# Hybrid decoder block on 8 cores: which pass over a weight tile leaves its bf16 copy behind

## The chip, the cores and the metric

One Trainium2 chip, all 8 of its cores. Each core works on 2 of the 16 sequences and no core waits for another, but they share the chip's memory. The time is device microseconds of the slowest core; a kernel's time is the median of its runs. Cores 0 to 3 are one die, 4 to 7 the other.

## The reference, cut to what matters

```python
def reference(x, meta_tokens, ...):          # x (16, 2048, 1024) float32
    h = concatenate([meta, x], axis=1)
    u = rms_norm(h, norm_mix_g) @ w_in       # (1024, 2576)
    c_val, c_gate, q, k, v, g, gate_lr = split(u)   # 512 512 256 256 512 512 16
    y_conv = silu(layer_norm(causal_conv31(c_val * sigmoid(c_gate))))
    y_gla = gated_linear_attention(q, k, v, decay(gate_lr))   # 4 heads, chunks of 64
    y_gla = head_norm(y_gla) * silu(g)
    h = h + concatenate([y_conv, y_gla], -1) @ w_out          # (1024, 1024)
    h = h + (silu(r @ w_gate) * (r @ w_up)) @ w_down, r = rms_norm(h, norm_ffn_g)   # 1024 -> 2816 -> 1024
    return rms_norm(h, norm_final_g)[:, 16:]
```

## The kernel before

A core's 4096 tokens are cut into 8 **blocks** of 512. A block goes through a mixer (`mixer`: convolution group, attention group, output projection) and a feed-forward part (`ffn`: 22 column groups j of gate and up, then the down projection). The feed-forward of a block is interleaved with the second part of the next block's mixer and the first part of the mixer after that. `plan` orders these pieces (`side` spreads them over a block by shares), each piece adds its instructions to `Prog`, and `Prog.schedule`, a list scheduler with estimated costs, sets the order on each engine by rank and readiness. After that each engine runs its list strictly in order. The queues of SyncE (SP) and GpSimd (POOL) also issue the DMAs: an instruction there that waits for a semaphore holds up all behind it.

**Weights.** All of them, 48 tiles of 128 x 2048, lie in memory as f32 (`wpack`, 1 MB a tile) and don't fit on chip, so each block loads every tile again, in a bf16 form of 512 KB in a slot of `wring`. Ring 0 (slots 0 to 3) serves the mixer (v, k, q, output gate, output projection; later the conv tiles too), ring 1 (slots 4 to 7) the feed-forward, and in block 0 the two first tensors of `h[2]` hold k and q (ring 2: wring8 and 9, printed as h_0 and h_1 or h2_0 and h2_1). `wget` hands out a slot, `wdone` frees it, and the freed slot is at once reloaded with the next tile of that ring's sequence (`wissue`). A reload waits for the last reader of the slot, be it TensorE or a store.

**Three kinds of load.** (a) A *cast*: GpSimd's queue reads the f32 tile and writes bf16 into the slot. (b) A cast followed by a *store*: SP's queue writes the slot to the bf16 copy `wsc` in memory. (c) A *read*: SP's queue reads `wsc`, once there is a copy. Tiles of `LATE_STORE` are cast twice and stored after the second cast; the others are cast once and stored at once. Tile numbers: 0 to 3 conv, 4 q, 5 k, 6 and 7 v, 8 and 9 output gate, 10 to 13 output projection, 14 to 24 gate (FG0 to FG10), 25 to 35 up (FU0 to FU10), 36 to 47 down (FD0 to FD11). Groups j = 2i and 2i+1 use FGi and FUi.

**Block 0.** The conv tiles' stores are put aside in `held_in` and written in the unit `ln`, after the convolution (`Bycv`). The tiles of rings 0 and 2 have a list `hold` of their own.

Lines that the rows name: L677 all products of eight steps (`mm8`: projections and gate/up; in the rows `ps<-x2T,wring` is gate/up, `ps<-wring,xT` v or output gate, `ps<-wring,yT` the output projection, `ps<-xT,wring` k, q or conv), L1297 the down projection, L449 a cast, L446 a read, L456 a store, L1249 the load of a block's tokens into `h`, L1333 the store of a finished block, L813 and L818 the way of the convolution's input through `vsc` into `rep`, L925 to L929 and L1024 GpSimd's part of the layer norm, L1122 its part of the attention state.

Of the kernel before, what the change touches and what calls it, by code (L numbers as in the profile page):

```python
# [28 lines left out]
NW = NWM + NWF  # L29
# [4 lines left out]

W_GATE, W_VAL, W_Q, W_K, W_V, W_G, W_O, W_FG, W_FU, W_FD = 0, 2, 4, 5, 6, 8, 10, 14, 25, 36
N_WT = 48
LATE_STORE = frozenset(t for t in range(N_WT) if W_Q <= t < W_O or (t >= W_FG and t % 3))

ORDER = (("start xt0 xt1 xt2 xt3 mt c0 c1 rep0 c2 c3 rep1 wcv z decay v0 v1 v2 v3 vm km conv0 k conv1 q ln g0 g1 g2 g3",
# [237 lines left out]
def build_program(nseq, seqlen):  # L277
# [25 lines left out]
    with es:  # L303
# [68 lines left out]
        def build(wseq):  # L372

            P = Prog()
            Bh = [[Buf(f"h{s_}_{t}") for t in range(NT)] for s_ in range(NH)]
# [32 lines left out]
            Bw = [Buf(f"w{i}") for i in range(NW)] + Bh[2][0:NWX]  # L408
# [26 lines left out]
                return ftmp[i], Bft[i]  # L435


            order, stored, loaded, freed, once = ([], [], []), set(), [0, 0, 0], (set(), set(), set()), set()
            RING = ((0, NWM), (NWM, NWF), (NW, NWX))

            def wissue(r, n, after=(), hold=None):
                tile, sl = wseq[r][n], RING[r][0] + n % RING[r][1]
                B_ = Bw[sl]
                dst = wring[sl][:]
                if tile in stored:
                    op = P.add("sp", lambda e: e.dma_start(out=dst, in_=wsc[tile]), R=[Bwsc[tile]], W=[B_], dkey=f"wh{sl}")  # L446
                    op.rank = (P.rank - 30.0, op.rank[1])
                else:
                    P.add("pool", lambda e: e.dma_start(out=dst, in_=wpack[tile]), R=after, W=[B_], dkey=f"wp{sl}")  # L449
                    if tile in LATE_STORE and tile not in once:  # L450
                        once.add(tile)
                        return
                    stored.add(tile)

                    def write(after=()):
                        P.add("sp", lambda e: e.dma_start(out=wsc[tile], in_=dst), R=[B_], A=after, W=[Bwsc[tile]], dkey=f"ws{sl}")  # L456
                    if hold is None:
                        write()
                    else:
                        hold.append(write)  # L460
# [13 lines left out]
            def wdone(o):  # L474

                if wseq is None:
                    return
                r = o.ring
                freed[r].update(range(o.first, o.first + len(o)))
                while loaded[r] in freed[r]:  # L480
                    n = loaded[r]
                    loaded[r] += 1
                    if n + RING[r][1] < len(wseq[r]):
                        wissue(r, n + RING[r][1])
# [3 lines left out]
            held_in, conv_w = [], {}  # L488

            def cload(dst, src, eng="sp", key=None):  # L490
                ncst[0] += 1
                P.add(eng, lambda e: e.dma_start(out=dst, in_=src), W=[Bc2(dst)], dkey=key or ("const" + eng))
# [19 lines left out]
                      W=[Bh[0][t]], dkey=f"h0_{t}")  # L512
            gain(gmix, g_mix_d, "gm")
            if wseq is not None:
                hold = []
                for r, n in [(1, 0), (1, 1), (1, 2), (1, 3)]:
                    wissue(r, n, after=[Bh[0][1]], hold=held_in)
            cload(wgl[:], wglp_d, eng="pool")
            if wseq is not None:
                for r, n in [(0, 0), (0, 1), (0, 2), (0, 3), (2, 0), (2, 1)]:  # L520
                    wissue(r, n, after=[Bh[0][1]], hold=hold)
                for write in hold:
                    write([Bw[NW + 1]])
            cload(wg2[:], wg2_d)
            cload(gb[:], gb_d)
            cload(convw4[:], convw4_d)
# [872 lines left out]
            n = sum(c for c, _ in pre)  # L1399
# [3 lines left out]
            n = sum(c for c, _ in post + late)  # L1403
# [5 lines left out]
            for b in range(nb):  # L1409
                units, fin = ffn(b % NH, blocks[b][0], b == 0, b == nb - 1)  # L1410
                n = sum(c for c, _ in units)
# [17 lines left out]
            return P, order  # L1429

        _, wseq = build(None)
        P, _ = build(wseq)
        nc.model_us = P.schedule()
        P.finalize()
# [95 lines left out]
```

How the kernel before makes its waits and increments, by code:

```python
    def emit(self, eng_name, eng, esem, dsem):  # L241
        seen = {}
        for b in self.ops[eng_name]:
            waits = {}
            for a in b.deps:
                if not self._needs_wait(a, b):
                    continue
                if a.dma:
                    s, v = dsem[a.dkey], (self.dcount[a.dkey] if a.dkey.startswith("const") else a.dval)
                else:
                    s, v = esem[a.eng], a.ticket
                k = id(s)
                if k not in waits or waits[k][1] < v:
                    waits[k] = (s, v)
            for k, (s, v) in waits.items():
                if seen.get(k, 0) >= v:
                    continue
                seen[k] = v
                eng.wait_ge(s, v)
            if b.fn is None:
                continue
            ins = b.fn(eng)
            if b.dma:
                ins.then_inc(dsem[b.dkey], 16)
            elif b.sig:
                ins.then_inc(esem[eng_name], 1)
```

## Time and profile before

| what | value |
|---|---|
| time, median of 3 runs (lowest, highest) | 1532.19 us (1531.98, 1574.51) |
| the profiled execution's own time, and its span | 1533.17 us, 1531.6 us |
| spans of the 8 cores | 1511.4 to 1531.6 us |
| TensorE busy; idle under L677 for casts, for reads (core 4) | 1433.6 us; 12.0 us, 8.6 us |
| DMA issues: casts, reads, stores of weight tiles | 77 (75 + 2 into `h[2]`), 303, 48 |
| to landing, median: cast, read, store | 9.5, 5.0, 6.1 us |
| memory read, written by one core | 276.22 MB, 46.40 MB |

The profile is of one execution and, without a core named, of core 4, whose span is the longest. The own time is 1.6 us over the span. "x31" is a count of instructions, a number in brackets the idle time before, with what ended it.

### The profile page before, as it was taken

How to read it: one execution, taken by the hardware profiler on the slowest of the kernel's cores; microseconds unless marked ns; L12 is line 12 of the kernel's file. 1: busy time of each engine (PE TensorE's matmuls, PEld its weight loads, DVE VectorE, ACT ScalarE, POOL GpSimd, SP SyncE). 2: the span in 40 equal slices, each digit the busy share in tenths (PEclk: the TensorE clock that was granted, in tenths of full speed). 3: DMA queues.
4: the chain of work that ended last, by engine and by line, in shares of the span. 5: the costliest groups of instructions: out<-in, count | busy, mean ns of one | idle time of the engine just before them, and what ended most of it. 6: DMA issues, size and time to landing. Idle time of an engine off the chain costs nothing.

```text
span 1531.6 us, 26341 instructions; the slowest of 8 cores (1511.4 to 1531.6 us)
## 1 busy us (share of the span) xinstructions
PE 1433.6 (94%) x8203; PEld 688.0 (45%) x8290; DVE 792.0 (52%) x1751; ACT 549.6 (36%) x976; POOL 266.5 (17%) x359
## 2 busy tenths in 40 slices
PE   4977899988999999999999999999999999999995
PEld 2444444434444444444444444444444444444442
DVE  3586275434654347545384356643484455744424
ACT  3654352434324344214523154223442145211102
POOL 2241240114201141002400133001410014000000
PEclk9989999999999999999999999999999999999998
DMA  9868997999878974497745985489744985375541
GB/s 193 215 169 197 184 212 172 203 236 258 215 208 236 247 227 150 146 219 241 213 145 173 210 273 166 147 200 232 244 154 143 219 239 174 114 211 178 187 163 55
DMA packets 128568, 297.55 MB, mean 194 GB/s; under 512 B 49056, under 2 KB 59680, under 8 KB 128432
## 3 DMA queue, kind: packets, MB, share of 16 engines
q1 hardware_dynamic: 66000, 199.92, 41.5%
q0 software_dynamic: 23904, 86.49, 25.8%
q10 hardware_dynamic: 38528, 9.44, 4.9%
q8 instruction: 70, 1.15, 0.3%
q14 instruction: 66, 0.54, 0.1%
HBM read 276.22 MB, written 46.40 MB: 211 GB/s over the span
## 4 chain that ended last, share of the span: by engine, by line
PE 79%; DMA 10%; issue 4%; ACT 4%; DVE 2%; POOL 0%; SPq 0%; DVEq 0%; ACTq 0%; POOLq 0%
PE ps L677 57%; PE ps L1297 17%; DMA wring<-wsc 4%; DMA wring<-wpack 4%; ACT yT L635 1%; PE ps L656 1%; PE ps L764 1%; PE ps L875 1%; DMA h<-xin 1%; DMA out<-h 1%; ACT rep L1030 0%; PE ps L1171 0%; PE ps L1198 0%; PE ps L1166 0%; PE ps L1069 0%
## 5 line engine op out<-in xcount | busy, mean ns | idle before, releaser
L677 PE MATMUL ps<-x2T,wring 128*128 128x512 bf16 (+1 forms) x2912 | 640.8, 374 | 21.7 <-DMA wring<-wsc 8.6
L677 PEld LDWEIGHTS ps<-x2T,wring 128*128 128x128 bf16 x2912 | 277.9, 98 | 345.7 <-issue 34.1
L1297 PE MATMUL ps<-wring,actT 128*128 128x512 bf16 x1368 | 305.6, 379 | 3.2 <-DMA wring<-wpack 1.0
L1281 DVE SCALAR_TENSOR_TENSOR ftmp<-ftmp,ps 128x512 f32<-128x512 f32 x176 | 120.7, 686 | 253.6 <-ACT ftmp L1280 253.3
L1280 ACT ACTIVATE ftmp<-ps 128x512 f32<-128x512 f32 x176 | 105.3, 599 | 353.4 <-PE ps L677 337.3
L1297 PEld LDWEIGHTS ps<-wring,actT 128*128 128x128 bf16 x1408 | 136.7, 98 | 168.7 <-issue 8.8
L677 PE MATMUL ps<-xT,wring 128*128 128x512 bf16 x736 | 165.9, 381 | 2.8 <-ACT xT L661 2.0
L1283 DVE SCALAR_TENSOR_TENSOR actT<-ftmp,ps 128x512 bf16<-128x512 f32 x176 | 120.1, 685 | 48.2 <-PE ps L677 43.8
L677 PE MATMUL ps<-wring,yT 128*128 128x512 bf16 x489 | 118.2, 383 | 7.9 <-issue 3.2
L677 PE MATMUL ps<-wring,xT 128*128 128x512 bf16 x488 | 115.5, 386 | 8.3 <-DMA wring<-wpack 4.8
L677 PEld LDWEIGHTS ps<-xT,wring 128*128 128x128 bf16 x736 | 71.7, 98 | 88.4 <-issue 5.8
L1024 POOL TENSOR_TENSOR rep<-rep,mtmp 128x512 f32<-128x512 f32 x60 | 77.2, 1287 | 41.6 <-ACT mtmp L932 27.5
L813 POOL DMA_DIRECT2D vsc<-vT x24 | 17.6, 732 | 379.1 <-DVE vT L798 377.0
L677 PEld LDWEIGHTS ps<-wring,yT 128*128 128x128 bf16 x512 | 49.5, 98 | 69.1 <-issue 12.3
L677 PEld LDWEIGHTS ps<-wring,xT 128*128 128x128 bf16 x512 | 49.4, 99 | 65.3 <-issue 12.2
L449 POOL DMA_DIRECT2D wring<-wpack x75 | 40.8, 547 | 211.7 <-PE ps L677 143.3
L786 ACT ACTIVATE mtmp<-ps 128x512 f32<-128x512 f32 (+1 forms) x32 | 17.8, 557 | 158.4 <-PE ps L677 131.6
L1030 ACT ACTIVATE rep<-rep,small 128x256 f32<-128x256 f32 x128 | 69.5, 592 | 5.1 <-POOL rep L1024 1.5
L798 DVE SCALAR_TENSOR_TENSOR vT<-mtmp,ps 128x256 bf16<-128x256 f32 x56 | 23.6, 421 | 88.4 <-PE ps L677 86.1
L1226 DVE TENSOR_TENSOR h<-h,ps 128x512 f32<-128x512 f32 x64 | 44.0, 687 | 46.6 <-PE ps L677 45.8
L1122 POOL TENSOR_TENSOR Rbd<-S,emid 64x256 bf16<-64x256 f32 x64 | 41.8, 653 | 144.7 <-DVE S L1116 63.9
L892 DVE TENSOR_TENSOR_SCAN csb<-ones,spb 128x128 f32<-128x128 f32 x64 | 27.4, 428 | 76.3 <-ACT spb L937 68.7
(190 smaller groups left out, 1229.1 us busy)
## 6 DMA issues: line engine op xcount, KB each, us to landing
wring<-wsc SPq DMA_DIRECT2D x303, 512.0 KB, 5.0
wring<-wpack POOLq DMA_DIRECT2D x75, 512.0 KB, 9.5
wsc<-wring SPq DMA_DIRECT2D x48, 512.0 KB, 6.1
h<-xin POOLq DMA_DIRECT2D x28, 512.0 KB, 12.7
out<-h POOLq DMA_DIRECT2D x28, 512.0 KB, 5.4
rep<-vsc POOLq DMA_DIRECT2D x24, 543.0 KB, 8.6
rep<-vsc SPq DMA_DIRECT2D x8, 543.0 KB, 7.7
yT<-rep SPq DMA_DIRECT2D x64, 64.0 KB, 3.5
```

The costliest lines, as they stand in the source:

```text
L449: P.add("pool", lambda e: e.dma_start(out=dst, in_=wpack[tile]), R=after, W=[B_], dkey=f"wp{sl}")
L677: ins = e.matmul(pt_ap, lhsT=lhs(kc), rhs=rhs(kc), start=(kc == 0), stop=(kc == KC - 1))
L798: P.add("dve", lambda e, pv=pv, th=th, a=a: e.scalar_tensor_tensor(out=vT[:, c, a, 16:16 + HT].rearrange("p (t m) -> p t m", t=NT), in0=ha ...
L892: P.add("dve", lambda e, i=i: e.tensor_tensor_scan(out=cs4[:, i, :], data0=ones[:], data1=sp4[:, i, :], initial=0.0, op0=ALU.mult, op1=ALU ...
L1024: P.add("dve" if bi == 0 and c % 2 else "pool", lambda e, src=src, op=op: e.tensor_tensor(out=y2, in0=y2, in1=src[:, 0:HT].unsqueeze(1).to ...
L1030: P.add("act", lambda e, r=r, k=k, dst=dst, fn=fn: e.activation(out=dst[:, r * HT:(r + 1) * HT], in_=y[:, r * HT:(r + 1) * HT], func=fn, s ...
L1122: P.add("pool", lambda e, t=t, hh=hh, rows=rows: e.tensor_tensor(out=Rbd[rows, t, :, hh, :], in0=S[rows, sl[t], :, :], in1=em2[rows, :, t] ...
L1226: P.add("dve", lambda e: e.tensor_tensor(out=hh_, in0=hh_, in1=pt[:], op=ALU.add), R=[Bpt, Bh[hs][t]], W=[Bh[hs][t]])
L1280: P.add("act", lambda e: e.activation(out=th[:], in_=pg[:], func=AF.Tanh, scale=0.5), R=[Bpg], W=[Bth])
L1281: P.add("dve", lambda e: e.scalar_tensor_tensor(out=th[:], in0=th[:], scalar=1.0, in1=pg[:], op0=ALU.add, op1=ALU.mult), R=[Bpg, Bth], W=[ ...
L1283: P.add("dve", lambda e: e.scalar_tensor_tensor(out=actT[:, j, :], in0=th[:], scalar=0.5, in1=pu[:], op0=ALU.mult, op1=ALU.mult), R=[Bpu, ...
L1297: ins = e.matmul(ps[t][:], lhsT=actT[:, j, t * 128:(t + 1) * 128], rhs=wd3[:, j - j0, :], start=(j == 0), stop=(j == NJ - 1))
```

## The change

k, q and the two output gate tiles leave `LATE_STORE`: they are cast once, stored in block 0 and read as bf16 from block 1 on. Their stores in block 0 join `held_in`, and the list `hold` goes. The new `THIRD_STORE` names every third tile of gate and up (FG0, FG3, FG6, FG9, FU1, FU4, FU7, FU10): these are cast three times, without a store in block 1, and stored after the third cast, in block 2. The counts of casts become 4 fewer in block 1 and 8 more in block 2.

```diff
-LATE_STORE = frozenset(t for t in range(N_WT) if W_Q <= t < W_O or (t >= W_FG and t % 3))
+LATE_STORE = frozenset(t for t in range(N_WT) if W_V <= t < W_G or (t >= W_FG and t % 3))
+THIRD_STORE = frozenset(t for t in range(W_FG, W_FD) if t % 3 == 2)
...
-            order, stored, loaded, freed, once = ([], [], []), set(), [0, 0, 0], (set(), set(), set()), set()
+            order, stored, loaded, freed, casts = ([], [], []), set(), [0, 0, 0], (set(), set(), set()), {}
...
-                    if tile in LATE_STORE and tile not in once:
-                        once.add(tile)
+                    if casts.get(tile, 0) < (tile in LATE_STORE) + (tile in THIRD_STORE):
+                        casts[tile] = casts.get(tile, 0) + 1
                         return
...
             if wseq is not None:
-                hold = []
                 for r, n in [(1, 0), (1, 1), (1, 2), (1, 3)]:
                     wissue(r, n, after=[Bh[0][1]], hold=held_in)
             cload(wgl[:], wglp_d, eng="pool")
             if wseq is not None:
                 for r, n in [(0, 0), (0, 1), (0, 2), (0, 3), (2, 0), (2, 1)]:
-                    wissue(r, n, after=[Bh[0][1]], hold=hold)
-                for write in hold:
-                    write([Bw[NW + 1]])
+                    wissue(r, n, after=[Bh[0][1]], hold=held_in)
```

The scheduler orders anew with this. Line numbers in the rows of the changed kernel are 1 higher up to L515 and 2 lower behind. Three places:

**GpSimd's queue where block 1's mixer gets its tiles** (wring0 and 1 take v, wring2 and 3 k and q, then wring0 and 1 the output gate; wring4 to 7 are FG2, FU2, FG3, FU3). Before:

```order
L449 DMA wring2<-wpack 128x2048 [waits dsem_wp2,dsem_ws2,sem_pe]
L449 DMA wring3<-wpack 128x2048 [waits dsem_wp3,dsem_ws3]
L449 DMA wring0<-wpack 128x2048 [waits dsem_wp0,dsem_ws0,sem_pe]
L449 DMA wring1<-wpack 128x2048 [waits dsem_wp1,dsem_ws1]
L449 DMA wring4<-wpack 128x2048 [waits dsem_wp4,sem_pe]
L449 DMA wring5<-wpack 128x2048 [waits dsem_wp5,sem_pe]
L449 DMA wring6<-wpack 128x2048 [waits dsem_wp6,dsem_ws6,sem_pe]
L449 DMA wring0<-wpack 128x2048 [waits dsem_wp0,dsem_ws0]
L449 DMA wring7<-wpack 128x2048 [waits dsem_wp7,sem_pe]
L449 DMA wring1<-wpack 128x2048 [waits dsem_wp1,dsem_ws1]
```

Now:

```order
L450 DMA wring0<-wpack 128x2048 [waits dsem_wp0,dsem_ws0,sem_pe]
L450 DMA wring1<-wpack 128x2048 [waits dsem_wp1,dsem_ws1]
L450 DMA wring4<-wpack 128x2048 [waits dsem_wp4,sem_pe]
L450 DMA wring5<-wpack 128x2048 [waits dsem_wp5,sem_pe]
L450 DMA wring6<-wpack 128x2048 [waits dsem_wp6,dsem_ws6,sem_pe]
L450 DMA wring7<-wpack 128x2048 [waits dsem_wp7,sem_pe]
```

The casts of k and q, ahead of v, and those of the output gate are gone; they are reads on SP's queue.

**TensorE at the same place**: gate/up of block 0 by 128 tokens (x2T 128x128), then v of block 1 (wring,xT) and gate/up by 512. Before:

```order
L656 MATMUL ps<-ident,xn_tm 128x128 x8
L677 MATMUL ps<-x2T,wring 128x128 x40
L677 MATMUL ps<-x2T,wring 128x512 x16
L677 MATMUL ps<-wring,xT 128x512 x32
L677 MATMUL ps<-x2T,wring 128x512 x16
L875 MATMUL ps<-rep,wcv 32x256 x128
```

Now:

```order
L654 MATMUL ps<-ident,xn_tm 128x128 x8
L675 MATMUL ps<-x2T,wring 128x128 x32
L675 MATMUL ps<-wring,xT 128x512 x24
L675 MATMUL ps<-x2T,wring 128x512 x16
L675 MATMUL ps<-wring,xT 128x512 x8
L675 MATMUL ps<-x2T,wring 128x512 x16
L873 MATMUL ps<-rep,wcv 32x256 x128
```

Three of the four v products now stand ahead of the gate/up products of 16, one behind.

**GpSimd's queue in block 2's feed-forward** (h1 is stored, then loaded with the tokens of a later block). Before:

```order
L1249 DMA h1_0<-xin 128x1024 [waits dsem_p1_0]
L1249 DMA h1_1<-xin 128x1024 [waits dsem_p1_1]
L1249 DMA h1_2<-xin 128x1024 [waits dsem_p1_2]
L1249 DMA h1_3<-xin 128x1024 [waits dsem_p1_3]
L925 TENSOR_TENSOR mtmp0<-rep 128x512 [waits sem_act,sem_pool]
L926 TENSOR_TENSOR mtmp1<-rep 128x512 [waits sem_act,sem_pool]
L927 TENSOR_TENSOR mtmp0<-mtmp0,mtmp1 128x512 [waits sem_pool]
```

Now:

```order
L1247 DMA h1_0<-xin 128x1024 [waits dsem_p1_0]
L1247 DMA h1_1<-xin 128x1024 [waits dsem_p1_1]
L1247 DMA h1_2<-xin 128x1024 [waits dsem_p1_2]
L450 DMA wring6<-wpack 128x2048 [waits dsem_wh6,sem_pe]
L1247 DMA h1_3<-xin 128x1024 [waits dsem_p1_3]
L923 TENSOR_TENSOR mtmp0<-rep 128x512 [waits sem_act,sem_pool]
L924 TENSOR_TENSOR mtmp1<-rep 128x512 [waits sem_act,sem_pool]
L925 TENSOR_TENSOR mtmp0<-mtmp0,mtmp1 128x512 [waits sem_pool]
L450 DMA wring5<-wpack 128x2048 [waits dsem_wh5,sem_pe]
L927 TENSOR_TENSOR mtmp0<-mtmp0 128x256 [waits sem_pool]
```

FG3 (wring6) now waits its turn behind the load of h1_2, and FU4 (wring5) stands inside the layer norm's sums.

## Rows read from the trace of the kernel before

**Rows 1.** The page: head and first part.

```profile
span 1531.6 us, 26341 instructions; the slowest of 8 cores (1511.4 to 1531.6 us)
...
PE 1433.6 (94%) x8203; PEld 688.0 (45%) x8290; DVE 792.0 (52%) x1751; ACT 549.6 (36%) x976; POOL 266.5 (17%) x359
```

**Rows 2.** Span and granted clock of core 5.

```profile
core 5: 1530.4 us, clock 0.983
```

**Rows 3.** Waits of PE, core 4: total us, times, longest.

```profile
PE ps L677 <- DMA wring<-wpack: 12.0, 3, 4.8
```

**Rows 4.** DMA queues from 90 to 100 us, core 4.

```profile
q0 software_dynamic: 288, 1.05, 62.5%
...
wring<-wpack POOLq DMA_DIRECT2D x2, 512.0 KB, 8.5
```

**Rows 5.** DMA in 40 slices, queue q1, 72 to 90 us, core 4.

```profile
DMA  2799200039999999999969939926241000000000
...
q1 hardware_dynamic: 886, 3.21, 55.8%
```

**Rows 6.** PE in time, core 4: start, us, instructions, idle before.

```profile
157.33 3.61 PE L677 MATMUL ps<-x2T,wring 128*128 128x512 bf16 x16 [1.57 <-DVE ftmp L1281]
165.70 8.19 PE L677 MATMUL ps<-wring,xT 128*128 128x512 bf16 x31 [4.76 <-DMA wring<-wpack]
```

**Rows 7.** PE in order of time at the same work, core 0.

```profile
155.21 3.61 PE L677 MATMUL ps<-x2T,wring 128*128 128x512 bf16 x16 [1.58 <-DVE ftmp L1281]
158.66 7.07 PE L677 MATMUL ps<-wring,xT 128*128 128x512 bf16 x32
```

**Rows 8.** GpSimd in order of time, core 4.

```profile
144.21 1.13 POOL L449 DMA_DIRECT2D wring<-wpack  x2 [5.38 <-PE ps L677]
145.94 1.09 POOL L449 DMA_DIRECT2D wring<-wpack  x2 [0.59 <-PE ps L677]
```

**Rows 9.** Landings of casts, core 4, issued from 143.5, then from 145.5.

```profile
DMA to landing us min/median/max: 6.6/8.4/10.2
...
DMA to landing us min/median/max: 14.7/16.7/18.7
```

**Rows 10.** Engines by stretch, core 4; PEclk is third from the end.

```profile
160.00:180.00 20.00, 15.24 (x152) 7.87 (x155) 2.75 (x4) 3.62 (x7) 2.12 (x4) 0.91 0.80 193
380.00:400.00 20.00, 18.93 (x81) 8.33 (x82) 10.07 (x16) 10.47 (x20) 7.78 (x7) 0.83 0.91 264
```

**Rows 11.** PE in order of time, core 4, second feed-forward part.

```profile
375.43 1.89 PE L677 MATMUL ps<-x2T,wring 128*128 128x512 bf16 x8
381.07 3.57 PE L677 MATMUL ps<-x2T,wring 128*128 128x512 bf16 x8 [3.75 <-DMA wring<-wpack]
```

**Rows 12.** PE in order of time, core 5, the same place.

```profile
374.94 3.18 PE L677 MATMUL ps<-x2T,wring 128*128 128x512 bf16 x8 [3.42 <-DMA wring<-wpack]
```

**Rows 13.** GpSimd in order of time, core 4, the same stretch.

```profile
363.14 1.15 POOL L449 DMA_DIRECT2D wring<-wpack  x2
365.47 0.53 POOL L1249 DMA_DIRECT2D h<-xin  x1 [1.18 <-DMA out<-h]
```

**Rows 14.** PE in order of time, core 4, third feed-forward part.

```profile
563.71 1.89 PE L677 MATMUL ps<-x2T,wring 128*128 128x512 bf16 x8 [0.83 <-DMA wring<-wsc]
...
566.71 1.89 PE L677 MATMUL ps<-x2T,wring 128*128 128x512 bf16 x8 [0.68 <-DMA wring<-wsc]
```

**Rows 15.** PE in order of time, core 5, third block.

```profile
562.39 2.91 PE L677 MATMUL ps<-x2T,wring 128*128 128x512 bf16 x8 [2.35 <-DMA wring<-wsc]
```

**Rows 16.** GpSimd in order of time, core 4, third block.

```profile
551.19 0.53 POOL L1249 DMA_DIRECT2D h<-xin  x1 [1.18 <-DMA out<-h]
```

**Rows 17.** Landings of L1249, core 4, issued 545 to 554.

```profile
DMA to landing us min/median/max: 7.6/11.6/14.3
```

**Rows 18.** DMA queues from 551 to 556 us, core 4.

```profile
q0 software_dynamic: 151, 0.55, 47.7%
q1 hardware_dynamic: 195, 0.73, 44.1%
```

## The prediction

> **What bounds the kernel now.** I read the page first: of a span of 1531.6 us TensorE is busy 1433.6, 94% [rows 1]. Its matmuls don't change in number, so the change can only move idle time, or the time at which matmuls run at a lower clock. Next the spans of the cores. The metric is the slowest core. Core 4 sets the span, but core 5 stands at 1530.4 us, 1.2 us behind [rows 2]. A gain that reaches core 4 alone is therefore worth at most 1.2 us. Then TensorE's waits on core 4: for casts 12.0 us in 3 waits [rows 3], nearly all in the first three blocks, where tiles are still cast. These waits are what the change can touch.
>
> **What a transfer costs.** From 90 to 100 us only two casts run on queue q0: 62.5% of 10 us in 288 packets, so 3.13 us of all 16 DMA engines and 144 packets for each [rows 4]. From 72 to 90 us queue q1 carries stores of 512 KB and a gain of the same size: 55.8% of 18 us is 10.04 us for 886 packets, or 6.15 transfers of 144, so 1.63 us each [rows 5]. A cast that becomes a read saves 1.5 us of DMA time, a store that goes saves 1.63.
>
> **Block 0, four more stores.** They go to SP's queue behind the four conv stores and ahead of gffn. The strip from 72 to 90 us shows the DMA engines idle from about 84.6 us (slice 28 of 40, 0.45 us each) [rows 5], and the next casts only run after 90. Four stores of 1.63 us are 6.5 us and end near 91. Queued behind them is gffn, which the second norm reads some 40 us later, and casts of wring2 and 3 may issue a little later on GpSimd. Cost 0. Without that gap it would be 6.5 us of DMA time ahead of the output projection's tiles.
>
> **Block 1, the v tiles.** On core 4 TensorE ends 16 gate/up matmuls (start 157.33, 3.45 us of work) near 160.8, then is idle for 4.76 us until v's second tile is there, and starts v at 165.70 [rows 6]. Core 0 does the same work with no wait at all, 158.66 right after 155.21 [rows 7]. GpSimd's queue issues k and q at 144.21 and v at 145.94 [rows 8]. They land 6.6 and 10.2 us after issue, v's 14.7 and 18.7 [rows 9]: at 150.8, 155.0, 160.6 and 165.2, so 4.8 us a cast while DMA is contended, against the 3.13 of before.
>
> Now v's casts are first in their queue. The first lands 6.6 us after 145.94, the second 4.8 later: 157.3 if the reads of k and q cost it nothing. If both reads go between them at the contended rate (1.63 x 4.8/3.13 = 2.5 us each) it is 162.3. The reads issue about 2 us ahead of v, so part of them is over by then; I take the middle, 159.8, and with the 0.5 us from landing to start v begins at 160.3. But in the new order v comes ahead of the 16 gate/up matmuls, so 3.45 us of work that used to fill the gap now follows: the equal of the old 165.70 is 163.75. Gain 1.95 us. Bounds: 162.3 gives a loss of 0.55, 157.3 or earlier (v at 157.33) a gain of 4.9.
>
> The clock adds to it. From 160 to 180 us the granted clock is 0.91, part of the time at 1.2 GHz in place of 2.4, after the wait [rows 10]. The 31 matmuls of v take 8.19 us [rows 6]; at core 0's pace of 7.07 for 32 they take 6.85 [rows 7], so 1.3 us. I give back half, 0.65, since a wait of about 3 us stays; bounds 0 and 1.8 (0.09 of 20 us). Core 4 gains 2.6 us here (-0.55 to 6.7). Core 0 and core 5 gain nothing: they don't wait here, or hardly. The output gate's two casts of this block save 3 us of DMA and four stores 6.5 us more, in a stretch in which TensorE doesn't wait: 0.
>
> **Block 1's feed-forward, eight stores fewer.** At 381.07 TensorE has waited 3.75 us for FU3, and its 8 matmuls then take 3.57 us, against 1.89 for the 8 before [rows 11]; the clock is 0.83 from 380 to 400 [rows 10]. Core 5 waits 3.42 us for the same tile [rows 12]. Before it, the stores of FG0 and FU1 go: 3.3 us of DMA time. Against that, FU3's cast, issued with FG3's from 363.14 on, ahead of a load at 365.47 [rows 13], now stands behind that load of 512 KB, 1.63 us. Net 1.6 us earlier, which I take for both cores. Bounds: the wait and all of the slow clock vanish (3.75 + 3.4 = 7.2 us), or the stores were over long before and the load counts alone (1.6 us lost). The other six stores go where no wait for a cast is seen.
>
> **Block 2, eight reads become casts, and eight stores come.** FG0 and FU1 are issued well ahead, while the down projection still runs, and the last three pairs fall where DMA is less loaded. The one that counts is FG3. Core 4 uses it at 563.71 after a wait of 0.83 us, and starts the second half of the group, with FU3, at 566.71 after another 0.68 [rows 14]; core 5 waits 2.35 us [rows 15]. As a cast FG3 is queued behind h1_2, issued at 551.19 [rows 16]. The loads of these four land 7.6 to 14.3 us after issue, median 11.6 [rows 17], so h1_2 at about 562.8 to 565.5, and FG3 3.13 us behind, at 565.9 to 568.6; middle 567.3. Both halves can then run together (FU3 is there): 567.8 + 3.45 = 571.2, against 566.71 + 1.7 = 568.4 before. Loss 2.8, with 0.2 for the clock: 3 us on either core. Bounds: a gain of 1.5 if FG3 comes as early as before (its waits gone), and 7 us if it lands at the late end (568.6 + 0.5 + 3.45 = 572.6 against 568.4, 4.2 us) and the slow clock costs nearly what it does at 381 (2.8 of 3.4 us).
>
> What do the queues share? From 551 to 556 us q0, with loads queued up, gets 47.7% and q1, with one or two reads, 44.1% [rows 18]. By the Trainium skill (DMA: Bandwidth & Descriptors, section SWDGE vs HWDGE vs iDMA) each DMA engine "round-robins between" the software and hardware queues; by that rule, the trace agrees, moving a tile from the queue with little in it to the long one costs its place. Were all served in the order of issue, FG3 would land near where it did and this term would be the 1.5 us of the longer transfer, and the sum 1.5 us lower.
>
> **The sum.** Core 4: 1531.6 - 2.6 - 1.6 + 3.0 = 1530.4. Core 5: 1530.4 - 0 - 1.6 + 3.0 = 1531.8. The slowest is now core 5, 0.2 us over the old span. The profiled execution's own time, 1533.17, is 1.6 over its span and 1.0 over the median of 1532.19, so a span stands for a time 0.6 higher: 1532.4. I forecast **1532 us**.
>
> **The rivals.**
> (1) *The second block gives back what the trace shows lost there.* If the freed DMA time ends both the wait at FU3 and its slow clock (on core 4 3.75 + 3.4 = 7.2 us, on core 5 3.42 + 3.4 = 6.8) and FG3's cast costs 3: core 4 is at 1531.6 - 2.6 - 7.2 + 3 = 1524.8, core 5 at 1530.4 - 6.8 + 3 = 1526.6, as a time 1527. With FG3 at its best bound too, core 5 is at 1530.4 - 6.8 - 1.5 = 1522.1, as a time 1523. For it: the wait follows a stretch full of transfers. Against: the queue order there gets worse. Chance 0.27.
> (2) *Slower: FG3's cast behind the loads of h1.* The mechanism is the one that the second block shows at 381: a cast in GpSimd's queue among loads of h. It decides as soon as FG3 lands later than 567.8 or so. With a loss of 7 us and the second block's term at 0: 1530.4 + 7 = 1537.4, as a time 1538; with 1.6 lost at FU3 as well, 1540. For it: core 5 waits here already with a plain read. Against: only two of the five tiles in this stretch are casts, FG3 and FU4, and FU4 has over 10 us in hand. Chance 0.25.
> (3) *Nothing arrives.* v's gain is used up by 340 us, since the stretch before it is bound by casts of the down projection that don't change, and FG3 finds the DMA free: 1531 to 1533, told from the forecast only by the trace. It counts with it.
>
> **Numbers.** Forecast with (3), 1529 to 1535: 0.46. (1) 1522 to 1529: 0.27. (2) 1535 to 1541: 0.25. Beyond: 0.02. The range 1523 to 1540 leaves out the last of both, under 0.2. 2% is 31 us, about what a measurement of this kernel tells from no change; no case comes near: faster 0.01, same 0.97, slower 0.02.
>
> **What would show it.** In the trace after: 79 casts and 299 reads among the issues of `wring`; stores in block 0 ending near 91 us with no new wait of TensorE behind; v on core 4 starting at 160 to 161 after a wait of some 3 us; at FU3 a wait of about 2 us; at FG3 a wait on `wpack` of 4 to 5 us near 567 on cores 4 and 5, less what came before. I am wrong if FG3 makes no wait, if the cores that don't wait for v today, such as core 0, come to wait for it since it is due 3.45 us earlier, or if the spans after block 2 differ by core for reasons of shared memory.

## The result and the profile after

The changed kernel took 1541.87 us (median of 20 runs), the kernel before 1536.69 us in 20 runs beside it. The ratio is 1.0039, 95% interval 1.0025 to 1.0054: about 6 us slower (4 to 8), outside the range of 1523 to 1540. Repeated in a later series it was 1.0036 (1.0003 to 1.0068). The times given are medians of all runs; the ratios leave out runs in which a die of cores ran slower at a lower granted clock, whatever the kernel, though one pair of cores at about 0.97 remains in some, the profiled runs of experiments 1, 2 and 4 among them.

Of the 9.9 us between the forecast of 1532 and this time, 4.5 are the kernel before's own: it took 1532.19 in the 3 runs that the forecast had, and 1536.69 in these 20. What the change did is the ratio.

The page of the changed kernel, profiled on core 3 (compare [rows 1]; before, on core 4, gate and up idled 21.7 us, the largest part of it, 8.6, for reads):

```profile
span 1534.5 us, 26419 instructions; the slowest of 8 cores (1520.7 to 1534.5 us)
...
PE 1444.0 (94%) x8290; PEld 690.9 (45%) x8290; DVE 790.0 (51%) x1751; ACT 549.5 (36%) x976; POOL 268.2 (17%) x363
...
L675 PE MATMUL ps<-x2T,wring 128*128 128x512 bf16 (+1 forms) x2912 | 645.0, 376 | 22.6 <-DMA wring<-wpack 16.8
...
wring<-wsc SPq DMA_DIRECT2D x299, 512.0 KB, 4.7
wring<-wpack POOLq DMA_DIRECT2D x79, 512.0 KB, 8.5
```

The kernel does what it says: 79 casts, 299 reads. Casts are now what ends most of the idle time of gate and up (16.8 of 22.6 us). But the page, of one execution and one core, hardly shows a loss (1531.6 to 1534.5 us). The cores must be seen side by side:

```profile
core 3: 1534.5 us, clock 0.981
core 4: 1521.7 us, clock 0.983
core 5: 1528.7 us, clock 0.982
```

Core 4, slowest before, is now 10 us faster, core 5 2 us faster, and core 3, at 1522.9 before, sets the time. The mean of the eight spans went from 1522.6 to 1526.9. So one needs a measure that all cores share.

**A measure by stages.** On each core the convolution group of a block is one row of 128 small matmuls in TensorE's list (L875 before, L873 after). Its start is a milestone. (In block 0 they are two rows of 64; the start of the second counts.) A step is the time from one block's milestone to the next. Core 5 of the changed kernel:

```profile
171.87 3.68 PE L873 MATMUL ps<-rep,wcv 128*32 128x256 bf16 x128
...
358.87 3.68 PE L873 MATMUL ps<-rep,wcv 128*32 128x256 bf16 x128
...
550.59 3.68 PE L873 MATMUL ps<-rep,wcv 128*32 128x256 bf16 x128
...
733.61 3.68 PE L873 MATMUL ps<-rep,wcv 128*32 128x256 bf16 x128
```

The steps from block 1 to block 4 are 187.0, 191.7 and 183.0 us. Block 1's v lies ahead of 171.87 on this core, FU3 of block 1 near 380, FG3 of block 2 near 568. The table has the median of the eight cores' steps, from one profiled run of each kernel; the last column has the ratio of times to the kernel before with its interval. The blocks that follow take 175 to 177 us a step in all kernels; single cores have longer steps, up to 180.0 us in the kernel before, 181.1 in the change and 186.5 in an experiment.

| kernel | block 0 to 1 | 1 to 2 | 2 to 3 (FU3, FG0) | 3 to 4 (FG3) | ratio |
|---|---|---|---|---|---|
| before | 102.1 | 184.2 | 189.5 | 176.6 | 1 |
| the change | 97.6 | 186.4 | 191.8 | 183.0 | 1.0039 (1.0025 to 1.0054) |
| first part only | 99.0 | 185.7 | 188.8 | 177.2 | 0.9965 (0.9922 to 1.0007) |
| third stores only | 106.4 | 186.0 | 191.0 | 182.6 | 1.0045 (1.0006 to 1.0083) |
| all but FG3 | 99.2 | 186.2 | 191.7 | 177.5 | 1.0019 (0.9980 to 1.0059) |
| first part and FG3 | 97.8 | 185.2 | 191.0 | 182.4 | 0.9981 (0.9951 to 1.0010) |
| first part, FG0, FU1 | 98.8 | 186.5 | 191.9 | 175.7 | 0.9994 (0.9967 to 1.0022) |
| first part, last four | 98.6 | 185.4 | 189.7 | 176.3 | 0.9976 (0.9954 to 0.9998) |
| FG3's cast first | 99.2 | 187.0 | 191.6 | 175.1 | 0.9955 (0.9905 to 1.0004) |
| loads behind FG3, FU3 | 98.6 | 187.5 | 187.4 | 175.3 | 0.9929 (0.9901 to 0.9957) |
| the same, again | 99.1 | 186.2 | 186.5 | 175.4 | 0.9933 (0.9910 to 0.9957) |
| the same, no third stores | 99.2 | 184.7 | 187.5 | 175.1 | 0.9955 (0.9932 to 0.9979) |
| before, loads behind | 104.1 | 184.2 | 186.8 | 175.1 | 0.9967 (0.9942 to 0.9991) |
| the change again | 98.6 | 187.4 | 190.6 | 183.8 | 1.0036 (1.0003 to 1.0068) |

Change against before: -4.5, +2.2, +2.3 and +6.4, together +6.4 us, and the measured ratio is +6.0. This sum is the result that has to be explained.

The table shows where time goes, but each row is one execution, and some sums of steps don't match their ratio. "First part and FG3" is 4.0 us over the kernel before by its steps and 2.9 under it by its ratio (7.5 under to 1.5 over). "Loads behind FG3, FU3" is 3.6 and 5.2 under by steps, 10.9 and 10.3 under by ratio. What makes the difference isn't shown.

**Block 1's v, and what is given back.** Core 4 after, TensorE in order of time (compare [rows 6] and [rows 11]):

```profile
153.35 3.38 PE L675 MATMUL ps<-x2T,wring 128*128 128x128 bf16 x32 [1.26 <-ACT x2T L662]
156.57 5.34 PE L675 MATMUL ps<-wring,xT 128*128 128x512 bf16 x24
161.75 3.62 PE L675 MATMUL ps<-x2T,wring 128*128 128x512 bf16 x16
165.21 1.89 PE L675 MATMUL ps<-wring,xT 128*128 128x512 bf16 x8
...
337.90 6.72 PE L675 MATMUL ps<-x2T,wring 128*128 128x512 bf16 x24 [5.32 <-DMA wring<-wpack]
...
370.02 1.89 PE L675 MATMUL ps<-x2T,wring 128*128 128x512 bf16 x8 [1.82 <-DMA wring<-wpack]
...
376.58 1.89 PE L675 MATMUL ps<-x2T,wring 128*128 128x512 bf16 x8 [2.51 <-DMA wring<-wpack]
```

v starts at 156.57 with no wait at all. The granted clock of core 4 is 1.00 from 160 to 180 us, against 0.91 before [rows 10]. No core of the eight waits for it. At 337.90 the wait for a feed-forward tile cast is 5.32 us, where core 4 waited 3.49 before; on the eight cores this wait is 3.3 to 7.2 us, before 1.9 to 3.9. Around 370 there are now two waits, FG3's and FU3's, where there was one.

**Block 2's FG3.** Core 5 after, TensorE in order of time (compare [rows 15]):

```profile
373.60 3.56 PE L675 MATMUL ps<-x2T,wring 128*128 128x512 bf16 x8 [3.17 <-DMA wring<-wpack]
...
568.27 3.52 PE L675 MATMUL ps<-x2T,wring 128*128 128x512 bf16 x8 [6.11 <-DMA wring<-wpack]
```

All eight cores wait for FG3: 4.84, 5.42, 4.69, 6.16, 5.40, 6.11, 5.96 and 6.51 us. GpSimd of core 5 shows why, in order of time and then as the landing of the cast of 551.10:

```profile
547.37 0.53 POOL L1247 DMA_DIRECT2D h<-xin  x1 [0.67 <-DMA out<-h]
548.94 0.53 POOL L1247 DMA_DIRECT2D h<-xin  x1 [1.04 <-DMA out<-h]
550.55 0.53 POOL L1247 DMA_DIRECT2D h<-xin  x1 [1.08 <-DMA out<-h]
551.10 0.53 POOL L450 DMA_DIRECT2D wring<-wpack  x1
```

```profile
DMA to landing us min/median/max: 16.8/16.8/16.8
```

Three loads were handed to the queue in the 4 us ahead of it, and it lands at 567.9, 4.7 us behind the last of the three. On the eight cores it takes 12.3 to 17.6 us to land, 3.7 to 4.7 of them behind that load. What that costs is best seen on core 1, which did not wait for a tile here before. Core 1 before, TensorE:

```profile
562.15 1.89 PE L677 MATMUL ps<-x2T,wring 128*128 128x512 bf16 x8 [0.27 <-DVE actT L1283]
563.88 0.59 PE L930 MATMUL ps<-mtmp,par 128*128 128x256 f32 x2
564.61 1.89 PE L677 MATMUL ps<-x2T,wring 128*128 128x512 bf16 x8
```

Core 1 after:

```profile
566.80 3.57 PE L675 MATMUL ps<-x2T,wring 128*128 128x512 bf16 x8 [5.42 <-DMA wring<-wpack]
570.17 1.06 PE L928 MATMUL ps<-mtmp,par 128*128 128x256 f32 x2
571.02 2.28 PE L675 MATMUL ps<-x2T,wring 128*128 128x512 bf16 x8
```

The granted clock of core 1 over these rows, before and after (third from the end, as in [rows 10]):

```profile
562.00:567.00 5.00, 4.71 (x22) 2.21 (x23) 1.37 (x4) 2.16 (x4) 1.59 (x2) 1.00 0.75 304
...
566.80:573.00 6.20, 6.20 (x18) 2.66 (x19) 1.11 (x2) 1.61 (x4) 1.04 (x1) 0.60 0.85 259
```

The wait is 5.42 us, against 0.27. Then the three rows take 6.50 us from the first start to the last end, against 4.35, at a granted clock of 0.60 in place of 1.00: 2.15 us. Together that is 7.3, and the step of core 1 grew by 7.3 (175.75 to 183.05).

### The profile page after: what moved, and what is told of

It reads as the page before. It is cut to its first block, busy times and chain, and to the rows that moved or that the text cites. A ratio compares the mean times of both kernels' runs of the same rounds, so it can differ in the third digit from the quotient of the medians.

```text
span 1534.5 us, 26419 instructions; the slowest of 8 cores (1520.7 to 1534.5 us)
## 1 busy us (share of the span) xinstructions
PE 1444.0 (94%) x8290; PEld 690.9 (45%) x8290; DVE 790.0 (51%) x1751; ACT 549.5 (36%) x976; POOL 268.2 (17%) x363
## 4 chain that ended last, share of the span: by engine, by line
PE 84%; DMA 9%; DVE 3%; issue 2%; ACT 1%; SPq 0%; DVEq 0%; ACTq 0%; POOL 0%; POOLq 0%
PE ps L675 61%; PE ps L1295 17%; DMA wring<-wpack 4%; PE ps L873 1%; DMA out<-h 1%; DMA vsc<-vT 1%; PE ps L654 1%; DMA gmix<-norm_mix_g 1%; DMA rep<-vsc 1%; DMA wring<-wsc 1%; PE ps L762 1%; DVE h L1328 0%; PE ps L1196 0%; PE ps L1169 0%; PE ps L1164 0%
## 5 line engine op out<-in xcount | busy, mean ns | idle before, releaser
L675 PE MATMUL ps<-x2T,wring 128*128 128x512 bf16 (+1 forms) x2912 | 645.0, 376 | 22.6 <-DMA wring<-wpack 16.8
L1295 PE MATMUL ps<-wring,actT 128*128 128x512 bf16 x1408 | 313.6, 382 | 3.1 <-DMA wring<-wpack 3.1
L1288 DVE TENSOR_TENSOR h<-h,ps 128x512 f32<-128x512 f32 x60 | 37.0, 678 | 61.3 <-PE ps L1295 61.3
L1224 DVE TENSOR_TENSOR h<-h,ps 128x512 f32<-128x512 f32 x64 | 43.9, 686 | 46.8 <-PE ps L675 46.3
```

Source lines behind the costliest of these rows:

```text
L675: ins = e.matmul(pt_ap, lhsT=lhs(kc), rhs=rhs(kc), start=(kc == 0), stop=(kc == KC - 1))
L1224: P.add("dve", lambda e: e.tensor_tensor(out=hh_, in0=hh_, in1=pt[:], op=ALU.add), R=[Bpt, Bh[hs][t]], W=[Bh[hs][t]])
L1288: P.add("dve", lambda e: e.tensor_tensor(out=hh_, in0=hh_, in1=ps[t][:], op=ALU.add), R=[Bps[t], Bh[hs][t]], W=[Bh[hs][t]])
L1295: ins = e.matmul(ps[t][:], lhsT=actT[:, j, t * 128:(t + 1) * 128], rhs=wd3[:, j - j0, :], start=(j == 0), stop=(j == NJ - 1))
```

## The experiments

All were timed in 5 rounds beside the kernel before. Their rows are in the table above.

**1. The first part alone.**

```diff
-THIRD_STORE = frozenset(t for t in range(W_FG, W_FD) if t % 3 == 2)
+THIRD_STORE = frozenset()
```

> THIRD_STORE is empty: only k, q and the output gate are stored in block 0 and read in block 1. Theory Q (the loss is FG3's cast in block 2, queued behind the loads of h1): no core waits for v in block 1, block 2's feed-forward is as before with waits for reads of 1 to 3 us near 565, so 0 to 4 us faster than the kernel before (ratio 0.997 to 1.000). Theory S (the first part itself costs, because the work that filled the gap at v is gone and the longer waits near 335 to 340 come from it): 1 to 4 us slower (1.001 to 1.003), with waits of 4 to 7 us near 338 on all cores.

1534.74 us, ratio 0.9965 (0.9922 to 1.0007). The steps are 99.0, 185.7, 188.8, 177.2: it keeps most of the gain at v, gives back 1.5 us up to block 2, and loses 0.6 where FG3 is used. The changed kernel's loss isn't from this part.

**2. The third stores alone**, in the kernel before: `THIRD_STORE` and the count of casts as in the change, `LATE_STORE` and `hold` as before.

> Only THIRD_STORE is added; k, q and the output gate are cast twice as before. Theory Q: the wait for FG3 near 565 is 4.7 to 6.5 us on every core and the time is 5 to 8 us over the kernel before (1.003 to 1.005), that is, at least the whole change's loss. Theory S: less than half of the change's loss, 0 to 3 us.

1549.02 us, ratio 1.0045 (1.0006 to 1.0083). Step 3 to 4 is 182.6, the same growth as in the change (183.0). All eight cores wait for FG3, 4.2 to 7.1 us. The waits for v are back on cores 1, 3, 4 and 7 (4.29, 3.31, 3.69, 3.69 us). The two parts add up: 0.9965 x 1.0045 = 1.0010, against 1.0039, within their wide intervals.

**3. The change without FG3's third cast.**

```diff
-THIRD_STORE = frozenset(t for t in range(W_FG, W_FD) if t % 3 == 2)
+THIRD_STORE = frozenset(t for t in range(W_FG, W_FD) if t % 3 == 2 and t != W_FG + 3)
```

> The whole change, but FG3 is stored after its second cast and read in block 2; seven tiles are cast a third time. Theory Q: the wait near 565 falls back to 1 to 3 us and the ratio to 0.998 to 1.001. Theory B (it is the bulk: every tile cast a third time adds a bit to the DMA load of block 2): 7/8 of the loss stays, ratio 1.003 or more.

1541.2 us, ratio 1.0019 (0.9980 to 1.0059). Step 3 to 4 falls from 183.0 to 177.5; step 2 to 3 stays at 191.7. By the trace one tile of eight carries the loss of that step. The ratio is above the 0.998 to 1.001 that theory Q had, and its interval can't tell a gain.

**4. FG3's third cast ahead of the loads.** All eight third casts stay. In block 2 the loads of h1 also wait until TensorE has let go of FG3's slot, so that the scheduler puts the cast first.

```diff
+third = tile == W_FG + 3 and casts.get(tile, 0) == 2
+if third: first_in.extend(B_.rd)
 op = P.add("pool", ... wpack[tile] ...)
+if third: op.rank = (P.rank - 30.0, op.rank[1])
...
 op = P.add("pool", ... h[hs][t] <- xin ...)
+if bi == 4: op.deps += [d for d in first_in if d not in op.deps]
```

> The whole change, but in block 2 FG3's cast is issued ahead of the four loads of h1, which wait with it for the slot. The same bytes move. Theory Q in its strict form (it is the place in GpSimd's queue, not the cast): the cast lands within 6 to 8 us of 551, no wait for it near 565, ratio 0.998 to 1.001. Theory L (a cast takes long in this stretch wherever it stands): a wait of 3 us or more stays, ratio 1.002 to 1.004.

1534.34 us, ratio 0.9955 (0.9905 to 1.0004), the change with one queue order mended. GpSimd of core 5, and the landing of the cast at 549.14:

```profile
549.14 0.53 POOL L455 DMA_DIRECT2D wring<-wpack  x1 [4.19 <-PE ps L682]
549.67 1.05 POOL L1254 DMA_DIRECT2D h<-xin  x2
551.25 0.53 POOL L1254 DMA_DIRECT2D h<-xin  x1 [0.53 <-DMA out<-h]
```

```profile
DMA to landing us min/median/max: 9.5/9.5/9.5
```

TensorE of core 5 at the two halves of the group:

```profile
561.62 1.89 PE L682 MATMUL ps<-x2T,wring 128*128 128x512 bf16 x8
563.35 0.59 PE L935 MATMUL ps<-mtmp,par 128*128 128x256 f32 x2
563.78 1.89 PE L682 MATMUL ps<-x2T,wring 128*128 128x512 bf16 x8
```

The same transfer lands 9.5 us after its issue in place of 16.8 (8.7 to 11.9 on the eight cores) and no core waits for it; step 3 to 4 is 175.1. So it is the place in the queue, not the f32 bytes of the tile. By its steps this kernel is 0.5 us over the one before, by its ratio 7 under (15 under to 1 over), where 3 under to 2 over was expected.

**5. FG3 alone.** The other end of experiment 3: `THIRD_STORE = frozenset((W_FG + 3,))`.

> The first block's part, and of THIRD_STORE only FG3: one tile is cast a third time. Theory Q: the step from conv to conv over block 2's feed-forward is 183 us on undisturbed cores, as in the whole change, with the wait of 5 to 6 us for FG3. Theory B (bulk of eight tiles): 177 to 178 us, one eighth of the way from the 177 of the first part alone.

1534.99 us, ratio 0.9981 (0.9951 to 1.0010). Step 3 to 4 is 182.4 with one tile, and all eight cores wait for it, 3.2 to 5.5 us. By that step the one cast costs 5.2 us against the first part alone, by the ratios 2.5 (0.9981 against 0.9965, with wide intervals). TensorE of core 4:

```profile
561.65 2.68 PE L675 MATMUL ps<-x2T,wring 128*128 128x512 bf16 x8 [4.44 <-DMA wring<-wpack]
```

**6. The loads of h behind FG3 and FU3 in every block.** The whole change; from block 1's feed-forward on, the loads of h wait for both slots, and both casts go first.

```diff
+if tile == W_FG + 3: first_in[:] = [d for d in B_.rd if d.eng == "pe"]
+if tile == W_FU + 3: first_in.extend(d for d in B_.rd if d.eng == "pe")
...
+if n >= 34 and tile in (W_FG + 3, W_FU + 3): op.rank = (P.rank - 30.0, op.rank[1])
...
+if bi > 2: op.deps += [d for d in first_in if d not in op.deps]
```

> The whole change, and in every feed-forward part from block 1 on the four loads of h wait for the slots of FG3 and FU3, whose casts or reads so are issued first. Theory Q: the waits at 370 to 380 in block 1 go too, the step over block 1's feed-forward falls by 3 us and that over block 2's to 175, ratio 0.993 to 0.997. Theory L (it is the load on the DMA engines, not the order): nothing beyond one block moves, 1.000 or more.

1527.38 us, ratio 0.9929 (0.9901 to 0.9957): 11 us faster than before. GpSimd of core 5 in block 1's feed-forward:

```profile
354.56 0.54 POOL L456 DMA_DIRECT2D wring<-wpack  x1 [3.65 <-PE ps L683]
356.28 0.53 POOL L456 DMA_DIRECT2D wring<-wpack  x1 [1.19 <-PE ps L683]
356.81 1.07 POOL L1255 DMA_DIRECT2D h<-xin  x2
```

TensorE of core 5, FG3 and FU3 of block 1:

```profile
367.04 1.89 PE L683 MATMUL ps<-x2T,wring 128*128 128x512 bf16 x8
368.77 0.59 PE L936 MATMUL ps<-mtmp,par 128*128 128x256 f32 x2
369.32 1.89 PE L683 MATMUL ps<-x2T,wring 128*128 128x512 bf16 x8
```

Neither waits, where core 5 waited 3.17 us for FG3 in the change and 3.42 for FU3 before [rows 12]. Step 2 to 3 falls from 191.8 to 187.4, which is below the kernel before's 189.5. Later groups wait instead on some cores (1.1 to 2.2 us near 385 to 394), for less.

**7. The kernel before with the same order of loads.**

> The kernel before with the same order of the loads of h, no change in what is cast or stored. If the place in the queue is a cost of its own, independent of the change: ratio 0.994 to 0.998, and the step over block 2's feed-forward is 175 us in place of 175 to 179. If e8 gains only by repairing the change, 0.999 to 1.001.

1532.25 us, ratio 0.9967 (0.9942 to 0.9991). The order is worth 5 us without the change too (1 to 9 by the interval, 2.2 by the steps); steps 2 to 3 and 3 to 4 are 186.8 and 175.1. On the same chip the change with this order was at 0.9929.

**8. The changed kernel again**, in the series of 5 to 7.

> The changed kernel itself, on the chip of the three others: ratio 1.002 to 1.006, the step over block 2's feed-forward 182 to 184 us on all eight cores with a wait for FG3's cast of 4.5 to 6.5 us.

1542.33 us, ratio 1.0036 (1.0003 to 1.0068), steps 98.6, 187.4, 190.6, 183.8. The loss and its place repeat. FG3's wait is 5.8 to 6.9 us on all eight cores, a little over what was expected.

**9. Only the last four third casts**: `THIRD_STORE = frozenset((W_FG + 6, W_FG + 9, W_FU + 7, W_FU + 10))`.

> The first part as changed; in the third block only FG6, FG9, FU7 and FU10 get third casts and stores, and FG3 is read as bf16 there. My theory (the loss sits in the cast of FG3 that is queued behind the loads of h1_0 to h1_2): without it the step from the third block's convolution to the fourth's goes back to about 177 us (176 to 178), and the ratio to the kernel before is 0.996 to 1.000. The rival (the third casts together cost it, by their bytes): four of eight would keep about half of the step's growth, 180 us, and the ratio is 1.000 to 1.002.

1534.48 us, ratio 0.9976 (0.9954 to 0.9998). Step 3 to 4 is 176.3, no growth from four tiles' bytes. TensorE of core 4 at FG3, here a read again and not waited for, and at FU3, a read in all of these kernels:

```profile
556.42 1.89 PE L675 MATMUL ps<-x2T,wring 128*128 128x512 bf16 x8
...
559.70 1.89 PE L675 MATMUL ps<-x2T,wring 128*128 128x512 bf16 x8 [0.96 <-DMA wring<-wsc]
```

**10. Only FG0 and FU1**: `THIRD_STORE = frozenset((W_FG, W_FU + 1))`.

> The first part as changed; third casts and stores of FG0 and FU1 alone, and FU3 behind the load of h0_2 in the second block. These two casts are issued at the start of the feed-forward. My theory: their waits near 518 to 526 us cost at most 1 us, so the step into the fourth block is 176 to 178 us; FU3 behind h0_2 keeps the step into the third block at 191 to 192 us (189 to 190 with FU3 ahead), and the ratio is 0.998 to 1.002. The rival (casts at any place cost as FG3's does): the step into the fourth block is above 180 us.

1534.75 us, ratio 0.9994 (0.9967 to 1.0022), steps 191.9 and 175.7. With these two, the scheduler puts FU3 of block 1 behind the load of h0_2, as in the change. In the six kernels in which it stands there (the change twice, experiments 2, 3, 4, 10) step 2 to 3 is 190.6 to 191.9; in the four with FU3 ahead of it (before, experiments 1, 5, 9) it is 188.8 to 191.0. The two casts are waited for 0.4 us at most, and add nothing that step 3 to 4 shows.

**11 and 12. The mended order without and with third stores**, side by side: experiment 6 with `THIRD_STORE = frozenset()`, and experiment 6 again.

> The first part as changed, no third stores, and in every feed-forward part from the second block on the loads of h stand behind the tiles FG3 and FU3. If third stores are worth nothing even with their casts ahead of the loads: the same as the next run, 0.992 to 0.995 of the kernel before. If the stores that move out of the second block help it: slower than the next run by 1 to 3 us. If the third casts still cost something: faster than it by 1 to 2 us.

> The whole change with the loads of h behind FG3 and FU3 in every feed-forward part from the second block on, run once more beside the one without third stores: 0.991 to 0.996 of the kernel before, the steps into the third and fourth block's convolutions 187 and 175 us.

1531.53 us, 0.9955 (0.9932 to 0.9979), and 1524.35 us, 0.9933 (0.9910 to 0.9957). Steps 2 to 3 and 3 to 4 are 187.5 and 175.1 without third stores, 186.5 and 175.4 with them. Once the loads are behind, third casts cost nothing; whether they gain 3 us can't be told from intervals this wide. The faster of the two is the best version found; its ratio repeated (0.9929 and 0.9933).

## Why the prediction was wrong, point by point

**The block 2 term is the step that failed.** It put "Loss 2.8, with 0.2 for the clock: 3 us on either core", and step 3 to 4 grew by 6.4 us. The mechanism was right: the forecast had FG3 landing between 565.9 and 568.6 and a wait of 4 to 5 us, and the trace has 567.9 on core 5 and 4.7 to 6.5. The size was wrong, by four things. First the clock, given as 0.2: the slow matmuls cost 2.15 us on core 1 and 1.4 on core 4 (3.26 against 1.89 for 8 matmuls). The price stood in [rows 11], where a wait of 3.75 us was followed by 3.57 for 8, and it was kept for the bound only. Second, FG3 was put 3.13 us behind the load of h1_2, the time of a cast while only two casts run [rows 4]; it landed 3.7 to 4.7 us behind it. Third, "Both halves can then run together" leaves out the two matmuls of L930 that stand between the halves, 0.4 us on core 4. Fourth, the sum took off what cores 4 and 5 already waited there before, 1.5 us on core 4 and 2.35 on core 5. Of the other six, three waited 0.6 to 1.2 us for a read and three for none. So the step grew by 3.8 on core 5, with its 2.35 us and slow clock before, by 5.1 on core 4, by 7.3 on core 1, and by up to 9.0 on the others. Experiments 3, 4, 5 and 9 show that this one cast, by its place, makes the growth.

**The block 1 feed-forward term had the wrong sign.** Forecast -1.6, by stores that go (3.3 us) less the load ahead of FU3 (1.6); step 2 to 3 grew by 2.3. The lower bound of the forecast, the load alone, was the one near the truth: FU3's cast landed 21.0 us after the convolution's start in the mean of the cores, 19.7 before. TensorE's order changed here too, which the forecast did not look at: FG3's 8 matmuls now stand ahead of 8 that need no feed-forward tile (`xT`). Core 5 before, ahead of the row of [rows 12]:

```profile
367.22 1.89 PE L677 MATMUL ps<-xT,wring 128*128 128x512 bf16 x8
...
369.63 1.89 PE L677 MATMUL ps<-x2T,wring 128*128 128x512 bf16 x8
```

Core 5 after, behind its wait for FG3 at 373.60:

```profile
377.44 1.89 PE L675 MATMUL ps<-xT,wring 128*128 128x512 bf16 x8
379.56 1.89 PE L675 MATMUL ps<-x2T,wring 128*128 128x512 bf16 x8 [0.23 <-DMA wring<-wpack]
```

So all eight cores now wait for FG3 too, 1.8 to 5.7 us, where two did before, and FU3's wait behind it is 0 to 3.2 us, before 0 to 4.8; the two together went from 3.2 to 4.9 us in the mean. In the rows of core 5 the two orders change together in experiments 2, 3, 4 and 10 as well, so what each costs was not separated. That the place ahead of the loads counts is shown by experiments 6 and 7: with FG3 and FU3 ahead of all loads the step is 187.4 and 186.8, and in experiment 6 FG3's matmuls stand ahead of those of `xT` too. That FU3's one place costs 2 us is weaker: experiment 5, with FU3 ahead, has 191.0. By core, the step grew by 3.2, 6.2 and 8.2 us on cores 1, 3 and 7 and moved by -0.9 (core 5) to 0.8 on the other five. So the 2.3 is a difference of medians, its sign doesn't hold for cores 4 and 5 that the sum followed, and its cause stays in part open.

**v.** Core 4: forecast start 160.3 and 2.6 us, measured 156.57 and 6.8 (block 1's convolution at 170.48, 177.27 before), the upper bound. The forecast had v's casts issued at 145.94, as before, behind those of k and q. With these gone they were issued at 144.45 and 145.04, after the reads of k and q (142.26, landed by 147.65), and landed at 151.5 and 155.6, ahead of the earliest case (157.3). So nothing waits, and the clock came back in full. Cores 0 and 5 reached block 1's convolution 1.1 us sooner and 1.4 later (168.0 against 169.1, 171.87 against 170.48), near the forecast's nothing. The fear that cores which did not wait would come to wait for v did not come true.

**The gain was not kept.** Of the 4.5 us at v, 2.2 are gone by block 2. The wait near 338 grew from 3.49 to 5.32 on core 4: the waits there are for casts, as rival (3) said of the way to 340 us. But the step 1 to 2 grew on every core, by 1.2 to 2.8 us on the four that had gained at v and by 1.7 to 5.7 on the four that had not, so it isn't only a gain handed back. The first part alone gives back 1.5. Which transfer takes the rest wasn't tried.

**The frame of the sum.** The forecast followed core 4 and core 5, since they were slowest in one execution, and capped core 4's gain at 1.2 us by core 5. But which core is slowest changes from run to run (core 3 after, core 5 or 6 in others), so the typical core counts. On it all terms apply: -4.5 + 2.2 + 2.3 + 6.4 = +6.4, a time of 1538.6. That is the place of **rival (2)**, 1538 to 1540, which had a chance of 0.25. Its mechanism and place were right, and its 7 + 1.6 us are near the 6.4 + 2.3 measured. That its time fits as well is in part luck: it starts from core 5, 1.2 us under the slowest, and leaves out the gain at v and what was given back, 2.3 us net. Still, "FG3's cast behind the loads of h1" should have been the forecast, with its own argument for it: the case that it decides "as soon as FG3 lands later than 567.8" was the one that the forecast's own middle (567.3) stood beside.

**Stores in block 0** cost 0, as forecast: nothing waits for them, though DMA is now busy to 90 us.

**Two queues side by side.** On core 5 after, GpSimd's transfers of 547.37 to 551.10 landed in the order of issue, at 557.66, 561.43, 563.27 and 567.92, but a read that SP issued at 550.75, behind the third of them, landed ahead of it, at 561.79. So what FG3 paid for was its place in GpSimd's queue: the same tile took 16.8 us to land behind the loads and 9.5 us ahead of them. By the Trainium skill (DMA: Bandwidth & Descriptors, section SWDGE vs HWDGE vs iDMA), as the prediction cites it, each DMA engine takes turns between the queues, and the trace agrees.

## What to carry to other kernels

When a transfer moves from a queue that is nearly empty to one that carries bulk loads, price it by its place in that queue, and look at whether its slot comes free before or after those loads are issued. Then put what is due first in front: that was worth 12 to 17 us against the changed kernel here by the ratios, and 6 to 12 by the steps. Price a wait of TensorE with the slow matmuls that followed a wait of its size in the same trace, and sum the terms over the typical core, since the slowest core of one profile is often not the slowest of the next.

## What was not expected of the hardware

Before the change exactly one core of each pair 0/1, 2/3, 4/5, 6/7 waited for v for more than 0.4 us: 1, 3, 4, 7. The stretch 152 to 164 us of the kernel before, by core (here 0, 1, 4 and 5; the last column is GB/s):

```profile
152.00:164.00 12.00, 10.42 (x71) 5.50 (x69) 4.04 (x6) 4.16 (x6) 1.06 (x2) 1.00 1.05 247
...
152.00:164.00 12.00, 6.98 (x71) 4.38 (x68) 4.29 (x7) 3.99 (x5) 1.06 (x2) 1.00 1.02 174
...
152.00:164.00 12.00, 6.54 (x64) 4.11 (x63) 4.03 (x6) 3.99 (x5) 1.06 (x2) 1.00 1.03 180
...
152.00:164.00 12.00, 9.53 (x67) 5.18 (x68) 4.03 (x6) 4.16 (x7) 1.06 (x2) 1.00 1.05 252
```

The DMA engines of both cores of a pair are busy nearly all the time (a share of 0.90 and more on all eight), but one moves 136 to 180 GB/s and its neighbour 247 to 252. In experiment 7, with the same mixer, the lesser ones were 0, 2, 5 and 7 (160, 176, 169, 177 GB/s against 232, 259, 229, 251), and these four reached block 1's convolution at 181 to 182 us, the others at 169 to 175. In experiment 2 the cores that waited were 1, 3, 4 and 7 again. What divides a pair this way, and what picks the lesser core, was not tested.
